# Moving the stationary tiles of the expert stage 64 bytes past a multiple of 512

## The chip, the core and the metric

The kernel runs on one core of one Trainium2 chip. Time is device time in microseconds (us) for one execution of the whole program, and the figure compared is the median of several executions. Times of single instructions are in nanoseconds (ns).

## What is computed

A two-layer encoder on 256 tokens of width 1024, all in float32. Each layer has a mixer with three branches; layer 0 then has a dense feed-forward block and layer 1 a mixture of eight experts. The change touches the expert part alone, so that is what has to be seen:

```python
def swiglu(h, w1, w3, w2):
    return (jax.nn.silu(h @ w1) * (h @ w3)) @ w2

def moe_ffn(h, router, w1, w3, w2):
    logits = (h @ router).astype(jnp.float32)
    top_v, top_i = lax.top_k(logits, TOP_K)
    top_w = jax.nn.softmax(top_v, axis=-1)
    gates = jnp.sum(jax.nn.one_hot(top_i, N_EXPERTS, dtype=jnp.float32) * top_w[..., None], axis=-2)
    y = gates[..., 0:1] * swiglu(h, w1[0], w3[0], w2[0])
    for e in range(1, N_EXPERTS):
        y = y + gates[..., e:e + 1] * swiglu(h, w1[e], w3[e], w2[e])
    return y
```

Every expert has w1 and w3 of 1024 x 3584 and w2 of 3584 x 1024, so the eight together are 336 pieces of 512 x 512 float32 (1 MiB each).

## The kernel before

**Precision.** Float32 products are made of three products of rounded parts. Each operand is split in a high part, rounded to the type fp32r, and a low part, the rest, in the same type. `mm3` (lines 1395 to 1399) multiplies high by high, high by low and low by high into one sum. The first tile argument of `pe.matmul` is the stationary one, which is loaded into the array (128 columns), the second is the moving one, which is streamed (512 columns in the expert stage). Each matmul has its own load of the stationary tile, also where the tile is the same as before.

**Expert stage.** A slot is up to 128 tokens of one expert. Here eight slots run: slot 0 written out, then a loop of seven. The weights of a slot come as 42 units (`UNITS`), each of 512 x 512. SyncE issues one DMA for each into a ring of 14 buffers `eraw` as soon as TensorE has finished the unit 14 before (`eunit_done`). ScalarE copies a unit to its high part `ehi` (line 830, three buffers), VectorE subtracts and writes the low part `elo` over the raw weights (line 1232). TensorE then runs four `mm3` for the unit (line 1736 for w1 and w3, the next branch for w2), 12 matmuls of 512 columns. The moving tiles are always the weights, `ehi` and `elo`. The stationary tiles are the tokens: `hehi` and `helo` (gathered tokens, written by lines 835 and 1277) for w1 and w3, and `eahi` and `ealo` (hidden activations, lines 860 and 1369; `ahi` and `alo` in the code) for w2. Between units TensorE transposes hidden activations (`turn`, line 1442, with the identity matrix held in `tab`), adds the result of the slot before to its tokens (`spread`, line 1711, moving tile `ysb`) and gathers the tokens of the next slot (line 1702, moving tile `Gm`).

**Layer 0 and both mixers.** They use the same `mm3`. In a feature unit (`feature_unit`) the weights are stationary and 256 token columns move; in a token unit (`token_unit`) the tokens `hhi`, `hlo` are stationary and the weights move, 512 or 448 columns of them. The router's product, ahead of the expert stage, has stationary tiles of 8 columns (`rhi`, `rlo`) and 256 moving columns.

**Placement.** All of SBUF that the kernel uses is one arena, whose base is rounded up to a multiple of 512 bytes. `keep` places permanent tiles one after another, each rounded up to 32 bytes; `w` places working tiles at written offsets from `work`, which is rounded up to a multiple of 512. `over_h` is the place of `hhi` (16,384 bytes in), which the expert stage reuses with `hlo` for `hid`, `eahi`, `ealo` and `ysb`. A stationary tile of 128 float32 columns is 512 bytes in each partition, so in the expert stage every tile that a load or a stream reads begins at a multiple of 512. The router's tiles are the exception: `rhi[:, k, :]` begins 32 k bytes past a multiple of 512, `rlo[:, k, :]` 256 bytes further.

Of the kernel before, what the change touches and what calls it, by code (L numbers as in the profile page):

```python
# [19 lines left out]
F32R = mybir.dt.float32r  # L20
# [5 lines left out]
P = 128  # L26
TOKENS, D, DEPTH = 256, 1024, 2
NB = TOKENS // P
KD = D // P
# [16 lines left out]
SLOT = P  # L46
# [97 lines left out]
def encoder(nc, ins, out):  # L144
    ctx = ExitStack()
    with ctx:
# [4 lines left out]
        def at(name, offset, shape, dtype=F32):  # L151
            size = 4
            for n in shape[1:]:
                size *= n
            assert offset + size <= arena_bytes, name
            return nc.alloc_sbuf_tensor_at(name, shape, dtype, offset=base + offset)

        place = [0]

        def keep(name, shape, dtype=F32):  # L160
            size = 4
            for n in shape[1:]:
                size *= n
            t = at(name, place[0], shape, dtype)
            place[0] += -(-size // 32) * 32
            return t
# [4 lines left out]
        over_h = place[0]  # L171
        hhi = keep("hhi", [P, KD, TOKENS], F32R)
        hlo = keep("hlo", [P, KD, TOKENS], F32R)
        tab = keep("tab", [P, T_W])
        bmask = keep("bmask", [P, HEADS, SCORE])
        mmask = keep("mmask", [P, SCORE])
# [17 lines left out]
        def w(name, offset, shape, dtype=F32):  # L194
            return at(name, work + offset, shape, dtype)
# [5 lines left out]
        o = 57344  # L201
# [53 lines left out]
        o = 57344  # L255
# [10 lines left out]
        o = 8192 * (RAW + HI)  # L266
# [3 lines left out]
        eraw = [w(f"eraw{i}", a, [P, 4, 512]) for i, a in enumerate(at_unit)]  # L270
        elo = [w(f"elo{i}", a, [P, 4, 512], F32R) for i, a in enumerate(at_unit)]
        o += 8192 * (E_GATES + E_MERGED)
        hehi = w("hehi", o, [P, KD, SLOT], F32R)
        helo = w("helo", o + 4096, [P, KD, SLOT], F32R)
        Gm = w("Gm", o + 8192, [P, NB, SLOT])
        Gg = w("Gg", o + 9216, [P, NB, SLOT])
        GT = w("GT", o + 10240, [SLOT, NB, P])
        o += 11264

        hid = [at(f"hid{i}", over_h + 2048 * i, [SLOT, FC]) for i in range(2)]  # L280
        ahi = [at(f"eahi{i}", over_h + 4096 + 2048 * i, [P, 4, SLOT], F32R) for i in range(2)]
        alo = [at(f"ealo{i}", over_h + 8192 + 2048 * i, [P, 4, SLOT], F32R) for i in range(2)]
        ysb = at("ysb", over_h + 12288, [SLOT, D])
        place[0] = work + o
        rhi = keep("rhi", [P, KD, NE], F32R)
        rlo = keep("rlo", [P, KD, NE], F32R)
# [1561 lines left out]
```

## Time and profile before

| | |
|---|---|
| median of three runs | 1732.25 us (1731.15 to 1734.08) |
| the profiled execution | 1730.65 us |
| its span, first to last instruction | 1728.8 us |
| TensorE busy (matmuls) | 1677.6 us, 97% |
| VectorE busy | 1270.7 us, 73% |
| ScalarE busy | 1053.4 us, 61% |
| read from HBM | 465.53 MB, 270 GB/s over the span |
| fp32r matmuls in the expert stage | 4032, from 710 to 1716 us |

All rows come from the profiled execution. PE is TensorE's matmuls, PEld its loads of stationary tiles, DVE VectorE, ACT ScalarE, SPq the queue of DMAs that SyncE issues. A matmul's recorded duration holds its way through the array, so consecutive ones overlap; what a matmul costs in a dense row is the distance from its start to the start of the next, called its spacing below. Names are written out<-in; for a matmul the output, then its two inputs, with the moving tile's form behind the array's size.

### The profile page before, as it was taken

To read this page: it belongs to the slowest core of one execution; us is meant where nothing else is said; L and a number is where in the kernel's file an instruction comes from. 1 tells how busy PE (TensorE), PEld (TensorE's weight loads), DVE (VectorE), ACT (ScalarE), POOL (GpSimd) and SP (SyncE) were. 2 spreads that over 40 slices of the span, in tenths; PEclk is the share of its full clock that TensorE was granted. 3 is DMA by queue.
4 is the path that set the end of the run, shared out by engine and by line. 5 is a ranking of instruction groups with operands and counts; after the bars stand their busy time and mean duration, and the time that the engine had idled before them with its cause. 6 is when DMAs were issued, how large, how long until landed. Compare 5 with 4: busy or idle time off the path is not lost.

```text
span 1728.8 us, 23259 instructions
## 1 busy us (share of the span) xinstructions
PE 1677.6 (97%) x9181; PEld 1438.4 (83%) x9181; DVE 1270.7 (73%) x991; ACT 1053.4 (61%) x950; POOL 18.7 (1%) x28
## 2 busy tenths in 40 slices
PE   5999999999899998899999999999999999999997
PEld 4899989999889997678888788788788788788786
DVE  4654565444566466798888888888898898898896
ACT  4364645433536454667667676776676776677675
POOL 1000000000000000000000000000000000000000
PEclk9999999999999999899999999999999999999999
DMA  6643454555654448899999999999999999999980
GB/s 235 208 145 124 147 195 147 183 185 174 209 174 145 137 152 296 313 349 372 323 357 377 316 362 364 323 365 355 327 373 342 337 371 338 344 370 338 346 299 24
DMA packets 234685, 468.52 MB, mean 271 GB/s; under 512 B 7552, under 2 KB 11744, under 8 KB 234624
## 3 DMA queue, kind: packets, MB, share of 16 engines
q1 hardware_dynamic: 232400, 459.17, 76.0%
q0 software_dynamic: 1936, 7.44, 1.2%
q8 instruction: 45, 0.74, 0.2%
q10 hardware_dynamic: 288, 1.05, 0.1%
q14 instruction: 16, 0.13, 0.0%
HBM read 465.53 MB, written 2.10 MB: 270 GB/s over the span
## 4 chain that ended last, share of the span: by engine, by line
PE 92%; DVE 4%; ACT 3%; DMA 1%; issue 1%; SPq 0%; DVEq 0%; ACTq 0%
PE big L1397 21%; PE big L1399 21%; PE big L1398 21%; PE small L1397 7%; PE small L1399 6%; PE small L1398 6%; PE small L1442 2%; DVE elo L1232 2%; PE small L1711 1%; ACT ehi L830 1%; PE small L1702 1%; DMA raw<-w_in 1%; PE small L1591 0%; PE small L1593 0%; PE small L1546 0%
## 5 line engine op out<-in xcount | busy, mean ns | idle before, releaser
L1232 DVE TENSOR_TENSOR elo<-eraw,ehi 128x2048 fp32r<-128x2048 f32 x336 | 769.1, 2295 | 106.5 <-ACT ehi L830 105.2
L830 ACT ACTIVATE ehi<-eraw 128x2048 fp32r<-128x2048 f32 x336 | 643.2, 1918 | 180.8 <-PE big L1399 136.8
L906 DVE TENSOR_TENSOR wlo<-raw,whi 128x2048 fp32r<-128x2048 f32 (+2 forms) x104 | 229.9, 2218 | 206.3 <-ACT whi L628 206.3
L1397 PE MATMUL big<-ehi,hehi 128*128 128x512 f32 x896 | 363.5, 406 | 1.4 <-DVE helo L1277 1.4
L628 ACT ACTIVATE whi<-raw 128x2048 fp32r<-128x2048 f32 (+2 forms) x104 | 192.5, 1858 | 269.8 <-PE big L1399 201.1
L1399 PE MATMUL big<-ehi,helo 128*128 128x512 f32 x896 | 350.0, 391 | 0.0
L1398 PE MATMUL big<-elo,hehi 128*128 128x512 f32 x896 | 349.4, 390 | 0.0
L1397 PE MATMUL big<-hhi,whi 128*128 128x256 f32 x864 | 248.1, 287 | 7.2 <-DVE hlo L926 7.0
L1398 PE MATMUL big<-hlo,whi 128*128 128x256 f32 x864 | 245.7, 284 | 0.0
L1399 PE MATMUL big<-hhi,wlo 128*128 128x256 f32 x864 | 245.7, 284 | 0.0
L1397 PEld LDWEIGHTS big<-ehi,hehi 128*128 128x128 f32 x896 | 168.3, 188 | 40.9 <-issue 5.1
L1398 PEld LDWEIGHTS big<-elo,hehi 128*128 128x128 f32 x896 | 168.5, 188 | 38.0 <-issue 5.0
L1399 PEld LDWEIGHTS big<-ehi,helo 128*128 128x128 f32 x896 | 168.2, 188 | 36.3
L1397 PE MATMUL small<-ehi,eahi 128*128 128x512 f32 x448 | 179.9, 402 | 4.0 <-DVE elo L1232 4.0
L1397 PEld LDWEIGHTS big<-hhi,whi 128*128 128x128 f32 x864 | 167.2, 193 | 10.5 <-DVE hlo L926 8.4
L1399 PE MATMUL small<-ehi,ealo 128*128 128x512 f32 x448 | 174.8, 390 | 0.0
L1398 PE MATMUL small<-elo,eahi 128*128 128x512 f32 x448 | 174.7, 390 | 0.0
L1398 PEld LDWEIGHTS big<-hlo,whi 128*128 128x128 f32 x864 | 167.1, 193 | 0.6 <-issue 0.5
L1399 PEld LDWEIGHTS big<-hhi,wlo 128*128 128x128 f32 x864 | 167.0, 193 | 0.0
L1397 PEld LDWEIGHTS small<-ehi,eahi 128*128 128x128 f32 x448 | 84.2, 188 | 27.1 <-DVE elo L1232 6.4
L1398 PEld LDWEIGHTS small<-elo,eahi 128*128 128x128 f32 x448 | 84.2, 188 | 18.1 <-issue 1.7
L1399 PEld LDWEIGHTS small<-ehi,ealo 128*128 128x128 f32 x448 | 84.1, 188 | 17.8
(292 smaller groups left out, 1698.2 us busy)
## 6 DMA issues: line engine op xcount, KB each, us to landing
eraw<-moe_w SPq DMA_DIRECT2D x336, 1024.0 KB, 5.1
raw<-ffn_w SPq DMA_DIRECT2D x30, 1024.0 KB, 5.0
raw<-w_gate SPq DMA_DIRECT2D x24, 1024.0 KB, 5.0
raw<-w_in SPq DMA_DIRECT2D x20, 1024.0 KB, 5.2
raw<-w_branch SPq DMA_DIRECT2D x12, 1024.0 KB, 4.9
raw<-w_o SPq DMA_DIRECT2D x8, 1024.0 KB, 5.1
raw<-w_in SPq DMA_DIRECT2D x4, 896.0 KB, 5.3
raw<-ffn_w SPq DMA_DIRECT2D x6, 512.0 KB, 3.7
```

The source lines that it names most:

```text
L628: act.activation(whi[u % HI][:, 0:kt, 0:cols], raw[u % RAW][:, 0:kt, 0:cols], ACT.Copy).then_inc(hi_ready, 1)
L830: act.activation(ehi[n % EHI][:, :, :], eraw[n % RING][:, :, :], ACT.Copy).then_inc(ehi_ready, 1)
L906: dve.tensor_tensor(wlo[u % RAW][:, 0:kt, 0:cols], raw[u % RAW][:, 0:kt, 0:cols], whi[u % HI][:, 0:kt, 0:cols].bitcast(F32), ALU.subtract) ...
L1232: dve.tensor_tensor(elo[n % RING][:, :, :], eraw[n % RING][:, :, :], ehi[n % EHI][:, :, :].bitcast(F32), ALU.subtract).then_inc(elo_ready, 1)
L1397: pe.matmul(o, sh, mh, start=start, stop=False, **kw)
L1398: pe.matmul(o, sh, ml, start=False, stop=False, **kw)
L1399: return pe.matmul(o, sl, mh, start=False, stop=stop, **kw)
L1442: return pe.transpose(o, src, ident[0:n, 0:n])
L1702: m = pe.matmul(small[:, gather_bank(s, i), SLOT * k:SLOT * k + SLOT], xn[:, b, (4 * i + k) * P:(4 * i + k + 1) * P], Gm[:, b, :], start=b ...
L1711: pe.matmul(small[:, 3, :], GT[:, i // 2, :], ysb[:, half:half + 512], start=True, stop=True).then_inc(spread_done, 1)
```

## The change

The stationary tiles of the expert stage are placed 64 bytes further: `hehi` and `helo` begin at `o + 64` and `o + 4160`, `eahi` and `ealo` at `over_h + 4160` and `over_h + 8256`, before and after the change each at a distance of 512 or 2048 from one another. `ysb`, the moving tile of `spread`, goes along with them to 64 past a multiple of 512. `Gm`, `Gg`, `GT` and what `keep` places behind them (`rhi` and on) move by a whole 512. To make room behind `ysb`, the permanent tables from `tab` to `rt` move by 64. `ehi`, `elo` and `eraw`, the moving ones, stay at multiples of 512. No instruction, wait, size or order changes.

```diff
@@ -171,6 +171,7 @@
         over_h = place[0]
         hhi = keep("hhi", [P, KD, TOKENS], F32R)
         hlo = keep("hlo", [P, KD, TOKENS], F32R)
+        place[0] += 64
         tab = keep("tab", [P, T_W])
@@ -270,17 +271,18 @@
         o += 8192 * (E_GATES + E_MERGED)
-        hehi = w("hehi", o, [P, KD, SLOT], F32R)
-        helo = w("helo", o + 4096, [P, KD, SLOT], F32R)
+        hehi = w("hehi", o + 64, [P, KD, SLOT], F32R)
+        helo = w("helo", o + 4160, [P, KD, SLOT], F32R)
+        o += 512
         Gm = w("Gm", o + 8192, [P, NB, SLOT])
         Gg = w("Gg", o + 9216, [P, NB, SLOT])
         GT = w("GT", o + 10240, [SLOT, NB, P])
         o += 11264
 
         hid = [at(f"hid{i}", over_h + 2048 * i, [SLOT, FC]) for i in range(2)]
-        ahi = [at(f"eahi{i}", over_h + 4096 + 2048 * i, [P, 4, SLOT], F32R) for i in range(2)]
-        alo = [at(f"ealo{i}", over_h + 8192 + 2048 * i, [P, 4, SLOT], F32R) for i in range(2)]
-        ysb = at("ysb", over_h + 12288, [SLOT, D])
+        ahi = [at(f"eahi{i}", over_h + 4160 + 2048 * i, [P, 4, SLOT], F32R) for i in range(2)]
+        alo = [at(f"ealo{i}", over_h + 8256 + 2048 * i, [P, 4, SLOT], F32R) for i in range(2)]
+        ysb = at("ysb", over_h + 12352, [SLOT, D])
         place[0] = work + o
```

## Rows read from the trace of the kernel before

**Rows 1.** The page's second part: 40 slices of the span, busy tenths of each.

```profile
PE   5999999999899998899999999999999999999997
PEclk9999999999999999899999999999999999999999
DMA  6643454555654448899999999999999999999980
```

**Rows 2.** Busy time by stretch (us, then busy us of each engine, clock, DMA).

```profile
740.00:1690.00 950.00, 946.41 (x4324) 772.53 (x4323) 823.49 (x530) 672.92 (x446) 0.00 (x0) 1.00 0.97 346
```

**Rows 3.** The same view, the busiest five us of DMA, where the ring is filled.

```profile
700.00:705.00 5.00, 3.81 (x17) 3.75 (x18) 2.62 (x8) 0.49 (x2) 0.00 (x0) 0.51 1.05 409
```

**Rows 4.** Waits, 740 to 1690 us: engine, line <- releaser: total us, times, longest.

```profile
ACT ehi L830 <- PE big L1399: 128.1, 198, 1.7
DVE elo L1232 <- ACT ehi L830: 97.2, 166, 1.1
...
PE small L1397 <- DVE elo L1232: 3.6, 10, 0.9
...
SPq L543 <- PE big L1399: 490.1, 208, 3.1
```

**Rows 5.** Timeline of PE in the expert stage (start us, us): 25 starts, first and last.

```profile
937.12 0.39 PE L1397 MATMUL big<-ehi,hehi 128*128 128x512 f32 x1
...
942.57 0.39 PE L1397 MATMUL big<-ehi,hehi 128*128 128x512 f32 x1
```

**Rows 6.** Timeline of PEld in the same stretch: the loads beside the matmuls.

```profile
937.81 0.19 PEld L1398 LDWEIGHTS big<-elo,hehi 128*128 128x128 f32 x1
938.04 0.19 PEld L1399 LDWEIGHTS big<-ehi,helo 128*128 128x128 f32 x1
```

**Rows 7.** Timeline of PE, a feature unit of 256 moving columns: 22 starts.

```profile
399.98 0.28 PE L1397 MATMUL big<-hhi,whi 128*128 128x256 f32 x1
...
402.50 0.28 PE L1397 MATMUL big<-hhi,whi 128*128 128x256 f32 x1
```

**Rows 8.** Timeline of PE, a token unit of 448 moving columns: nine starts.

```profile
59.83 0.36 PE L1397 MATMUL big<-whi,hhi 128*128 128x448 f32 x1
...
61.45 0.36 PE L1399 MATMUL big<-whi,hlo 128*128 128x448 f32 x1
```

**Rows 9.** Timeline of PE, the router's product: stationary tiles of eight columns.

```profile
692.66 0.28 PE L1397 MATMUL small<-hhi,rhi 128*8 128x256 f32 x1 [2.21 <-issue]
692.78 0.28 PE L1398 MATMUL small<-hlo,rhi 128*8 128x256 f32 x1
692.89 0.28 PE L1399 MATMUL small<-hhi,rlo 128*8 128x256 f32 x1
693.01 0.28 PE L1397 MATMUL small<-hhi,rhi 128*8 128x256 f32 x1
693.13 0.28 PE L1398 MATMUL small<-hlo,rhi 128*8 128x256 f32 x1
693.25 0.34 PE L1399 MATMUL small<-hhi,rlo 128*8 128x256 f32 x1
```

**Rows 10.** Timeline of PE, plain float32 matmuls in a row (xcount, merged).

```profile
98.95 3.40 PE L1546 MATMUL small<-cqnT,wuq 128*128 128x256 f32 x15
849.39 1.02 PE L1711 MATMUL small<-ysb,GT 128*128 128x512 f32 x2
87.15 0.82 PE L1442 MATMUL small<-tab,csb 128*128 128x128 f32 x6
1074.45 1.95 PE L1702 MATMUL small<-Gm,xn 128*128 128x128 f32 x16
```

**Rows 11.** Groups of instructions, 740 to 1690 us: writers of weights and stationary tiles.

```profile
L830 ACT ACTIVATE ehi<-eraw 128x2048 fp32r<-128x2048 f32 x318 | 609.1, 1918 | 170.8 <-PE big L1399 128.1 <-PE small L1399 42.8
L1232 DVE TENSOR_TENSOR elo<-eraw,ehi 128x2048 fp32r<-128x2048 f32 x319 | 728.6, 2290 | 98.4 <-ACT ehi L830 97.2
L1369 DVE TENSOR_TENSOR ealo<-small,eahi 128x512 fp32r<-128x512 f32 x53 | 36.4, 687 | 22.0 <-ACT eahi L860 22.0
L1277 DVE TENSOR_TENSOR helo<-small,hehi 128x512 fp32r<-128x512 f32 x14 | 9.6, 687 | 5.6 <-ACT hehi L835 5.6
```

## Prediction

> **What bounds the kernel now.** I read first the 40 slices of the page, then the busy time by stretch, then the waits, and last the timeline of TensorE alone, because the change alters nothing but addresses and only the timeline shows what one access costs. The slices say that TensorE is at nine tenths nearly everywhere and its clock at full speed, 2.4 GHz [rows 1]. In the heart of the expert stage it is busy for 946.4 of 950 us at a granted clock of 1.00, beside DMA at 0.97 of its time and 346 GB/s [rows 2]. Two engines look full there, so the waits decide. Each DMA issue waits for TensorE to finish a unit (490 us in the larger of two groups), ScalarE waits for TensorE to free a buffer of the high part (128 us), VectorE waits for ScalarE (97 us), and TensorE waits for VectorE for a few us in all [rows 4]. DMA is therefore paced by TensorE; it has been seen at 409 GB/s while the ring was filled [rows 3]. TensorE is the bound, and the expert stage is 4032 matmuls of fp32r, 12 for each of 336 units. Whatever a placement does to one of them is multiplied by 4032.
>
> **What one of them costs.** From the start at 937.12 to the one 24 later at 942.57 lie 5.45 us, a spacing of 227.1 ns [rows 5]. At 2.4 GHz 512 columns take 213.3 ns, so 13.8 ns are on top. The load of the next stationary tile begins within 0.01 us of a matmul and lies wholly under it (0.19 us recorded) [rows 5, 6], so its reading and the streaming run side by side. The same sum elsewhere, all with loads of 128 columns and at the same residue modulo 512: 256 moving columns come every 2.52 / 21 = 120.0 ns, 13.3 above their 106.7 [rows 7], and 448 every 1.62 / 8 = 202.5 ns, 15.8 above their 186.7 [rows 8]. Plain float32 matmuls are streamed at half the rate. Their 15 with 256 columns are (3.40 - 0.38) / 14 = 215.7 ns apart, where 213.3 would be the bare stream (0.38 is the recorded duration of one) [rows 10]. So a stream of fp32r pays some 11 ns per matmul that a float32 one with an equal load does not. This is what the change can reach, if reading both tiles from the same place modulo 512 is its cause.
>
> **Is it the cause?** The trace has one test of it. The router's product loads 8 columns and not 128, and its tiles begin at 0, 256, 32 and 288 bytes past a multiple of 512 in turn, with the moving tile at 0. Its starts at full clock, 692.66 to 693.25, give 0.59 / 5 = 118 ns, every single one 110 to 120 as far as two decimals tell [rows 9]. That is 11.3 ns above the stream of 106.7. A load with a sixteenth of the reads keeps 11.3 of the 13.3 ns, and four different residues give the same. A collision of the two reads should have shrunk with the load, or changed with the residue. What goes with the load's length is 13.3 - 11.3 = 2 ns. Against this weighs that 64 is not among the four residues, that all four might fall on the same banks, and that 8 columns are a short load. The row nearest to the disputed thing speaks for a fixed cost of changing the stationary tile under a fast stream, so I take nothing.
>
> **The change part by part.** Removed and added instructions: none; DMAs and waits: none; queue orders: the same.
> The stationary tiles at residue 64, 4032 matmuls: taken as 0. Lower bound: all that fp32r pays above float32, 227.1 - 215.7 = 11.4 ns each [rows 5, 10], 4032 x 11.4 = 46 us. Upper bound: the worst addition seen for any fp32r stream, 15.8 - 13.3 = 2.5 ns [rows 7, 8], 4032 x 2.5 = 10 us.
> The identity in `tab`, now at 64, moving tile of each transpose: they are (0.82 - 0.27) / 5 = 110 ns apart, where a gather of the same size without transposing takes (1.95 - 0.27) / 15 = 112 [rows 10]. The bare stream is 106.7, so with the 224 of the hidden activations and some 200 others between -1.4 and +0.8 us; I take 0.
> `ysb` at 64, moving tile of 56 matmul records in the loop, of which two take 1.02 us, their starts 0.43 apart [rows 10]. The bare stream is 427 ns, so nothing can be gained; an fp32r-like charge of 11 ns would be 0.6 us. I take 0.
> Writes of the moved tiles: the low part of activations and that of the gathered tokens take 687 ns each, though they lie in two different regions [rows 11]. Copies of 512 columns do not feel where they land, and DMA touches none of the moved tiles but small tables once. Tables from `tab` to `rt` already begin at assorted multiples of 32 (the three behind `tab` at 96 past a multiple of 512, by their sizes), so ScalarE and VectorE read such addresses now. 0.
> The sum is 1730.65 + 0 = 1730.65 us for the profiled execution, with its small terms -1.4 to +1.4. The median of the runs is 1.6 us above that execution, so the forecast is 1732 us.
>
> **A rule weighed.** The rows show 227.1 ns for a spacing with a load wholly beside it [rows 5, 6]. The Trainium skill, page TensorE: Matmul & The Clock Gate, section on what each phase of a matmul is for, says that TensorE has two independent read ports and that "Loading the next tile's weights doesn't steal SBUF read bandwidth from the running matmul." By that rule the placement does nothing and the sum stays 1732. The same page, section Wait — 56ns, not 53.3ns?, puts the fixed cost of a warm matmul at 2.5 ns, an estimate of 215.8 ns for 512 columns; the float32 row agrees, the fp32r rows do not, by 11 ns. If those 11 ns were a theft the first rule denies, the sum would be the faster rival's.
>
> **Rival 1, faster: the reads do collide.** Load and stream begin together at the same residue in every one of the 4032, and the fp32r stream reads twice as many bytes in a microsecond as the float32 one, which pays next to nothing. If a shift of 64 bytes keeps the two on different banks, up to 11.4 ns go. For it: the gap between fp32r and float32, and that no residue of 64 has been timed. Against it: the 8-column row. What is late next: a buffer freed by TensorE takes 1.92 + 2.29 = 4.21 us through ScalarE and VectorE [rows 11], and TensorE meanwhile has two units of 12 x 227.1 ns = 2.73 us, 5.45 us; at 215.7 ns it would have 5.18, still 0.97 to spare. VectorE needs 2.29 us and its smaller work out of the 3.0 us that a unit now takes on average (950 / 318), and 2.9 would do. DMA would have to give 346 x 3.0 / 2.86 = 363 GB/s, against the 409 seen. So nearly all of it arrives; I take off 2 us for the few places where TensorE already waits for VectorE [rows 4] and have 46 - 2 = 44 us: 1688 us. A partial gain, the 2 ns that do go with the load's length, would be 8 us: 1724 us.
>
> **Rival 2, slower: the load now crosses a boundary.** A stationary tile of 512 bytes at a multiple of 512 lies in one block of that size; 64 bytes on it reaches into two, on all 4032 loads. If fetching a second block costs as the odd length of 448 columns seems to cost the stream, 2.5 ns come on top, 10 us in all: 1742 us. It decides from 0.9 ns a matmul on (3.5 us). For it: lengths that are no multiple of 256 columns do pay [rows 8]. Against it: the load is hidden for all but the start of the next matmul, and the router's loads at 32 and 288 are no slower.
>
> **Rival 3: the change does not do what it says.** The base is rounded to 512 and the working tiles' offset stays at 45,056 by the sizes, so the residues are as written. Were the placement undone, the time would be 1732 too; I count it with no change.
>
> **How the numbers follow.** No change, 0.42, with its own range 1730 to 1735. Faster, 0.38: two thirds of it near the full 1688, the rest between it and 1728. Slower, 0.20: three quarters at 1736 to 1746 around 1742, the rest beyond, since a collision that equal residues happen to avoid has no row that bounds it. About 0.2%, 3.5 us, is what a measurement of this kernel can tell from no change. The range 1686 to 1746 holds the three cases but for that last piece and the deepest gains.
>
> **What would show it.** In the expert stage the spacing between consecutive starts is the whole test: 227 ns for no change, 216 for the full collision, about 225 for the part, 229.6 for the crossing. The layers before must be the same to within a us: their spacing 227, 120 and 202.5. The transposes at 110 and the spread at 0.43 us show whether `tab` and `ysb` matter. If the spacing falls and the time does not, TensorE's waits for `elo`, or issues of SPq that no longer wait for TensorE, say which of the two took its place. The prediction is wrong at its root if the spacing moves by more than a ns.

## The result and the profile after

The changed kernel takes 1751.08 us (median, 1749.98 to 1752.79) against 1731.70 us for the kernel before. The ratio is 1.0111, 95% interval 1.0094 to 1.0129: slower by 1.1%, some 19 us, outside the range given. Its profiled execution has a span of 1750.1 us, 21.3 more than before.

The page's first two rows of slices and the busy time by stretch (us, then busy us and count of each engine, clock, DMA share, GB/s) of the changed kernel:

```profile
PE   5999999999999997999999999999999999999997
PEclk8999999999999999999999999999999999999999
...
740.00:1690.00 950.00, 947.29 (x4239) 756.59 (x4238) 808.11 (x521) 659.12 (x436) 0.00 (x0) 1.00 0.98 343
```

TensorE is as busy as before and its clock as full, but in the 950 us of the expert stage it ran 4239 matmul records and not 4324 [rows 2]. Nothing new waits. Of the waits of the same stretch (engine, line <- releaser: total us, times, longest) those for TensorE grow, and behind them that of VectorE for ScalarE (108.2 for 97.2 us), while TensorE waits for VectorE for less than before (2.7 for 3.6 us, [rows 4]):

```profile
ACT ehi L832 <- PE big L1401: 137.9, 194, 1.7
DVE elo L1234 <- ACT ehi L832: 108.2, 168, 1.1
...
PE small L1399 <- DVE elo L1234: 2.7, 10, 0.7
```

The cause stands in the timeline of TensorE, 25 starts of the changed kernel (first and last), which answer to [rows 5]:

```profile
911.23 0.39 PE L1399 MATMUL big<-ehi,hehi 128*128 128x512 f32 x1
...
916.83 0.39 PE L1399 MATMUL small<-ehi,eahi 128*128 128x512 f32 x1
```

That is 5.60 / 24 = 233.3 ns where it was 227.1. The writers of the moved tiles did not change (687 and 688 ns for the low parts, [rows 11]). Where the whole time went is seen from the first and the last matmul of the low weights (duration ns min/median/max, first and last start us), the first two rows before, the last two after:

```profile
L1398 PE MATMUL big<-elo,hehi x896: 387/389/398, 710.7 to 1700.0; 128*128 128x512 f32 x180
L1398 PE MATMUL small<-elo,eahi x448: 387/389/398, 733.6 to 1715.6; 128*128 128x512 f32 x150
```

```profile
L1400 PE MATMUL big<-elo,hehi x896: 388/394/398, 711.8 to 1721.1; 128*128 128x512 f32 x180
L1400 PE MATMUL small<-elo,eahi x448: 392/394/398, 734.9 to 1736.8; 128*128 128x512 f32 x150
```

The stage was 1715.6 - 710.7 = 1004.9 us and is 1736.8 - 711.8 = 1025.0, so 20.1 of the 21.3 us lie in it, 5.0 ns for each of 4032 matmuls; the other 1.1 us lie ahead of it. It is 5.0 and not 6.2 for two reasons. The 25 starts read before were among the quickest: over the whole stage, taking from the starts every spacing below 240 ns, the mean was 227.8 and is 233.3 ns, 5.5 more. And the spacings from 240 ns on, where TensorE pauses or does other work between units, shrank a little, from 57.7 us in all (135 of them) to 54.1 (126). The median recorded duration rose with the spacing, from 389 to 394 ns. A grouped row can show that, but it marks a spacing of 233 ns alone: a kernel further below has 229.2 ns at a median of 388.

### The profile page after: what moved, and what is told of

Its sections match the earlier page's. It is cut to its first block, busy times and chain, and to the rows that moved or that the text cites. A ratio compares the mean times of both kernels' runs of the same rounds, so it can differ in the third digit from the quotient of the medians.

```text
span 1750.1 us, 23259 instructions
## 1 busy us (share of the span) xinstructions
PE 1699.0 (97%) x9181; PEld 1439.4 (82%) x9181; DVE 1272.0 (73%) x991; ACT 1053.9 (60%) x950; POOL 18.7 (1%) x28
## 4 chain that ended last, share of the span: by engine, by line
PE 92%; DVE 3%; ACT 2%; DMA 1%; issue 0%; SPq 0%; DVEq 0%; ACTq 0%
PE big L1399 21%; PE big L1400 21%; PE big L1401 21%; PE small L1399 7%; PE small L1400 7%; PE small L1401 7%; PE small L1444 2%; DVE elo L1234 2%; PE small L1713 1%; ACT ehi L832 1%; PE small L1704 1%; DMA raw<-w_in 1%; PE small L1593 0%; PE small L1595 0%; PE small L1548 0%
## 5 line engine op out<-in xcount | busy, mean ns | idle before, releaser
L1399 PE MATMUL big<-ehi,hehi 128*128 128x512 f32 x896 | 367.2, 410 | 1.4 <-DVE helo L1279 1.4
L1401 PE MATMUL big<-ehi,helo 128*128 128x512 f32 x896 | 353.8, 395 | 0.0
L1400 PE MATMUL big<-elo,hehi 128*128 128x512 f32 x896 | 353.7, 395 | 0.0
```

Of the source, the lines that this page charges most:

```text
L1399: pe.matmul(o, sh, mh, start=start, stop=False, **kw)
L1400: pe.matmul(o, sh, ml, start=False, stop=False, **kw)
L1401: return pe.matmul(o, sl, mh, start=False, stop=stop, **kw)
```

## Experiments

Two theories stood first. R: what counts is how the residue of the stationary tile stands to that of the moving one. B: the stationary tile reaches over a boundary of 512 bytes and its load costs more, as the slower rival had it. s and m below are the bytes by which the stationary and the moving tile lie past a multiple of 512.

### A bench of residues

Not the encoder. Its engine program runs rows of 40 matmuls of fp32r, in the order high, high, low of the stationary tile and high, low, high of the moving one, each with its own load. While the rows run no other engine works and the DMA share is 0.00. It ran once.

```python
for i in range(ROUNDS):
    k = i // 3
    lo = (0, 0, 1)[i % 3]
    ml = (0, 1, 0)[i % 3]
    a = P * (k % 2 + 2 * lo) + s % 32 // 4
    b = 512 * (k % 2 + 2 * ml) + m % 32 // 4
    q = pe.matmul(ps[c % 2][0:ld, 0:cols], st[:, a:a + ld], mv[:, b:b + cols], ...)
```

> Not the encoder: a bench that only runs rows of 40 fp32r matmuls with their loads, one row for each pair of residues modulo 512 of stationary tile (s) and moving tile (m); its output is not the reference's. Theory R (what counts is the difference of the two residues): s=0 m=0 gives a spacing of 227 ns for 512 columns, s=64 m=0 gives 233, s=64 m=64 and s=256 m=256 give 227 again, and s=0 m=64 differs from 227 too. Theory B (a stationary tile that reaches over a boundary of 512 costs more, whatever moves): every s other than 0 gives 233, s=64 m=64 too, and every m with s=0 gives 227. With loads of 8 columns both expect s=0 and s=64 within 1 ns of each other if the cost goes with the load's length; if the cost is paid at the start of the two reads, 8 columns show it in full.

The timeline of its TensorE; a row is (start us, time of all, moving and stationary tile named by their residue, stationary columns, moving columns, count). A spacing is (time of all - 0.39) / 39, 0.39 being the recorded duration of one.

```profile
33.27 9.23 PE L88 MATMUL ps<-m0x,s0x 128*128 128x512 f32 x40
42.34 9.24 PE L88 MATMUL ps<-m0x,s16x 128*128 128x512 f32 x40
51.41 9.49 PE L88 MATMUL ps<-m0x,s32x 128*128 128x512 f32 x40
60.74 9.50 PE L88 MATMUL ps<-m0x,s64x 128*128 128x512 f32 x40
...
79.43 9.44 PE L88 MATMUL ps<-m0x,s128x 128*128 128x512 f32 x40
88.71 9.32 PE L88 MATMUL ps<-m0x,s192x 128*128 128x512 f32 x40
97.87 9.24 PE L88 MATMUL ps<-m0x,s256x 128*128 128x512 f32 x40
106.95 9.49 PE L88 MATMUL ps<-m0x,s320x 128*128 128x512 f32 x40
...
144.06 9.31 PE L88 MATMUL ps<-m64x,s0x 128*128 128x512 f32 x40
...
180.94 9.48 PE L88 MATMUL ps<-m448x,s0x 128*128 128x512 f32 x40
190.26 9.25 PE L88 MATMUL ps<-m64x,s64x 128*128 128x512 f32 x40
...
255.97 9.40 PE L88 MATMUL ps<-m0x,s0x 128*8 128x512 f32 x40
265.21 9.43 PE L88 MATMUL ps<-m0x,s64x 128*8 128x512 f32 x40
274.48 9.36 PE L88 MATMUL ps<-m0x,s0x 128*64 128x512 f32 x40
283.68 9.47 PE L88 MATMUL ps<-m0x,s64x 128*64 128x512 f32 x40
```

At m=0 the stationary residues 0, 16 and 256 give 226.7 to 226.9 ns, 32, 64 and 320 give 233.3 to 233.6, 128 gives 232.1 and 192 gives 229.0. With s=0, a moving residue of 64 gives 228.7, as s=192 does, and 448 gives 233.1, as s=64 does. Equal residues of 64 give 227.2. Rows of the same s - m modulo 256 agree within 1.5 ns throughout, and s=0 and s=64 run again at the end give 227.2 and 233.3. So the spacing goes by s - m, and it repeats every 256 bytes: theory R. B falls, since equal residues of 64 reach over the boundary and cost nothing. The bench has the encoder's 227 and 233 with no DMA and no other engine at work, so those have no part in it. The last four rows concern the test on which the prediction rested. With loads of 8 columns the spacing is 231.0 at s=0 and 231.8 at s=64: it hardly feels the residue, and it is higher than the 226.7 of a full load. With 64 columns it is 230.0 and 232.8. So what the residue of 64 costs does grow with the load, 0.8, 2.8 and 6.9 ns for 8, 64 and 128 columns, while the spacing at equal residues falls.

### Both kinds of tile at 64

```diff
-        ehi = [w(f"ehi{i}", 8192 * i, [P, 4, 512], F32R) for i in range(EHI)]
+        ehi = [w(f"ehi{i}", 64 + 8192 * i, [P, 4, 512], F32R) for i in range(EHI)]
...
-        at_unit = [o + 8192 * i for i in range(E_GATES + E_MERGED)]
-        at_unit += [8192 * (EHI + i) for i in range(RING - E_GATES - E_MERGED)]
+        at_unit = [64 + o + 8192 * i for i in range(E_GATES + E_MERGED)]
+        at_unit += [64 + 8192 * (EHI + i) for i in range(RING - E_GATES - E_MERGED)]
...
```

> The changed kernel with ehi, elo and eraw at 64 past a multiple of 512 too, so that stationary and moving tiles have the same residue again and each stationary tile still reaches over a boundary of 512. Theory R (difference of residues): spacing back at 227 ns, 1732 us. Theory B (boundary of the stationary tile): spacing stays at 233 ns, 1751 us.

1731.91 us against 1731.00, ratio 1.0003 (0.9994 to 1.0013). The whole loss is gone while every stationary tile still lies at 64. The median recorded duration is back at 389 ns, and the spacings below 240 ns average 228.1. In the encoder too it is the relation of the two.

### The stationary tiles back, the rest left moved

`hehi`, `helo`, `eahi`, `ealo` at multiples of 512; `tab` and what follows it, and `ysb`, stay at 64. Against the changed kernel:

```diff
-        hehi = w("hehi", o + 64, [P, KD, SLOT], F32R)
-        helo = w("helo", o + 4160, [P, KD, SLOT], F32R)
+        hehi = w("hehi", o, [P, KD, SLOT], F32R)
+        helo = w("helo", o + 4096, [P, KD, SLOT], F32R)
...
-        ahi = [at(f"eahi{i}", over_h + 4160 + 2048 * i, [P, 4, SLOT], F32R) for i in range(2)]
-        alo = [at(f"ealo{i}", over_h + 8256 + 2048 * i, [P, 4, SLOT], F32R) for i in range(2)]
+        ahi = [at(f"eahi{i}", over_h + 4096 + 2048 * i, [P, 4, SLOT], F32R) for i in range(2)]
+        alo = [at(f"ealo{i}", over_h + 8192 + 2048 * i, [P, 4, SLOT], F32R) for i in range(2)]
```

> The changed kernel with hehi, helo, eahi and ealo back at multiples of 512; the tables from tab on and ysb stay at 64 past one. Theories R and B both: spacing 227 ns, 1732 us. Theory T (the moved tables or the spread's moving tile are to blame): 1745 us or more with a spacing near 227 in the dense rows.

1731.21 us, ratio 1.0000 (0.9990 to 1.0009). Tables, identity and `ysb` cost nothing that can be measured, as the prediction's small terms had it.

### Only the gathered tokens moved

The lower half of that edit alone: `eahi` and `ealo` back at multiples of 512, `hehi` and `helo` at 64.

```diff
-        ahi = [at(f"eahi{i}", over_h + 4160 + 2048 * i, [P, 4, SLOT], F32R) for i in range(2)]
+        ahi = [at(f"eahi{i}", over_h + 4096 + 2048 * i, [P, 4, SLOT], F32R) for i in range(2)]
...
```

> The changed kernel with eahi and ealo back at multiples of 512, hehi and helo at 64 past one: two thirds of the 4032 matmuls keep the moved stationary tile. Both R and B: 6 ns on 2688 of them, 16 us less what waits hide, so 1745 us; the matmuls into small (w2) at 227 ns, those into big at 233.

1746.01 us, ratio 1.0085 (1.0068 to 1.0101): 15.0 us for two thirds of the matmuls, where 16 less what waits hide were expected. The rows of this kernel show the two kinds side by side, w1 and w3 with the longer duration, w2 with the old one (their spacings below 240 ns average 233.3 and 228.5):

```profile
L1400 PE MATMUL big<-elo,hehi x896: 391/394/398, 712.0 to 1715.5; 128*128 128x512 f32 x180
L1400 PE MATMUL small<-elo,eahi x448: 387/389/402, 735.0 to 1731.1; 128*128 128x512 f32 x150
```

### The roles swapped

The moving tiles at 64 as in the kernel with both kinds at 64, the stationary ones at multiples of 512:

```diff
-        hehi = w("hehi", o + 64, [P, KD, SLOT], F32R)
-        helo = w("helo", o + 4160, [P, KD, SLOT], F32R)
-        o += 512
+        hehi = w("hehi", o + 512, [P, KD, SLOT], F32R)
+        helo = w("helo", o + 4608, [P, KD, SLOT], F32R)
+        o += 1024
...
```

> The changed kernel with the roles swapped: ehi, elo and eraw at 64 past a multiple of 512, hehi, helo, eahi and ealo at multiples of 512. If any unequal residues cost the same: 233 ns, 1751 us. If the signed difference s - m modulo 256 counts, as the first bench has it (192: 228.9 ns against 227.2 at 0): 4032 times 1.7 ns, 7 us on 1731, so 1738 us.

1735.89 us against 1731.65, ratio 1.0027 (1.0017 to 1.0036). The loss is 4 us and not 19: the sign of the difference counts. The stage shows it too:

```profile
L1400 PE MATMUL big<-elo,hehi x896: 387/388/398, 710.8 to 1705.1; 128*128 128x512 f32 x180
L1400 PE MATMUL small<-elo,eahi x448: 387/388/398, 733.8 to 1720.7; 128*128 128x512 f32 x150
```

It lasts 1720.7 - 710.8 = 1009.9 us, 5.0 more than before, and its spacings below 240 ns average 229.2 ns, as the bench's rows at 192 do, against 227.8 before. That is 1.4 ns, 5.6 us on 4032 matmuls; the 7 us expected took 1.7 ns from the bench, whose own 226.7 to 227.2 at equal residues the encoder does not quite reach.

### 256 in place of 64

Tables, stationary tiles and `ysb` at 256 past a multiple of 512:

```diff
-        place[0] += 64
+        place[0] += 256
-        hehi = w("hehi", o + 64, [P, KD, SLOT], F32R)
+        hehi = w("hehi", o + 256, [P, KD, SLOT], F32R)
...
```

> The changed kernel with 256 in place of 64: stationary tiles, ysb and tables 256 past a multiple of 512. Difference modulo 256: 0, spacing 227, 1732 us. A rule modulo 512, or a boundary of 512 that is crossed: 233 ns, 1751 us.

1730.81 us against 1731.51, ratio 0.9996 (0.9986 to 1.0006). The encoder repeats every 256 bytes as the bench does.

### A bench of lengths, and tiles that alternate

The same bench with other residues and numbers of columns, and two rows in which the residues alternate from one matmul to the next:

```diff
-                st, mv = views["s", s], views["m", m]
                 for i in range(ROUNDS):
+                    s, m = both(ss)[i % 2], both(ms)[i % 2]
+                    st, mv = views["s", s], views["m", m]
```

> A second bench, no encoder, its output is not the reference's: rows of 40 fp32r matmuls, stationary residues in steps of 16 bytes at m=0 for 256 and 512 moving columns, some other lengths, and two rows that alternate. If the spacing depends on the difference s - m modulo 256, s=0 m=64 at 256 columns equals s=192 m=0. Alternating tiles tell which pair counts. Row (s0 with m0, s64 with m64): 227 ns if a matmul's own two tiles count, and about 231 (the mean of 233.4 and 228.9) if what counts is the load that runs beside a stream, which is the load of the next matmul. Row (s64 with m0, s0 with m64): about 231 if the own pair counts, 227 if the load beside the stream counts. For 256 columns the first bench gave 113.7 at s=64 and 120 at 0 and 256; a theory that every unequal residue costs expects no value below 120 elsewhere.

At 512 columns the finer steps show a shelf and not a slope: 0 and 16 at 226.9, everything from 32 to 160 between 232.1 and 234.4, 192 at 229.2, 224 at 233.3. The rows of 256 columns, for which 0.28 us is the duration of one:

```profile
24.29 4.95 PE L94 MATMUL ps<-m0x,s0x 128*128 128x256 f32 x40
...
33.81 4.89 PE L94 MATMUL ps<-m0x,s32x 128*128 128x256 f32 x40
...
43.26 4.70 PE L94 MATMUL ps<-m0x,s64x 128*128 128x256 f32 x40
...
62.09 4.96 PE L94 MATMUL ps<-m0x,s128x 128*128 128x256 f32 x40
...
71.69 4.87 PE L94 MATMUL ps<-m0x,s192x 128*128 128x256 f32 x40
```

Here equal residues are among the worst, (4.95 - 0.28) / 39 = 119.7 ns, and s=64 the best, 113.3; 192 gives 117.7. With 192, 320 and 384 columns all four residues tried lie within 3.5 ns of one another, and equal ones cost no more than 0.7 ns over the best. At 448 columns 192 is the best, 200 ns against 203 at equal residues, and at 480 it is 64, 216 against 217. The two alternating rows begin at 326.72 and 335.98 and the next row at 345.31:

```profile
326.72 0.40 PE L94 MATMUL ps<-m0x,s0x 128*128 128x512 f32 x1
...
335.98 0.39 PE L94 MATMUL ps<-m0x,s64x 128*128 128x512 f32 x1
...
345.31 0.40 PE L94 MATMUL ps<-m0x,s0x 128*128 128x512 f32 x1
```

The row whose own pairs are equal takes 9.26 / 40 = 231.5 ns, as it should if what counts is the load that runs beside a stream, which is that of the next matmul. Its two kinds of start differ as that reading wants, 233.5 ns on average from a stream at 0 and 229.5 from one at 64. The opposite row should then have 227 and takes 9.33 / 40 = 233.3, which neither reading gives. For tiles that alternate the rule is open; the difference is a rule for rows of constant residues. So that load and stream get in each other's way is the likely reason for it, but no run shows it.

### The gain of 256 columns, in the mixer

The kernel before, with one line more; `work` stays at a multiple of 512, so the expert stage keeps equal residues. Feature units then have s - m = 64 modulo 256, token units 192.

```diff
         over_h = place[0]
+        place[0] += 192
         hhi = keep("hhi", [P, KD, TOKENS], F32R)
```

> The kernel before with hhi and hlo at 192 past a multiple of 512 and the expert stage as before. In feature units s - m is then 64 modulo 256, for 2592 matmuls of 256 columns; in token units it is 192 for 576 of 448 or 512. Theory of the difference, with the bench's figures: 2592 times 6.2 ns gained, 576 times 1.7 lost, so 15 us faster, 1716 us, spacing 113.7 in feature units. Rival, that any departure from equal residues costs in a real kernel: 1732 or more. Rival, that the weights' path bounds these units: spacing 113.7 within a unit and the time unchanged.

1722.12 us against 1731.65, ratio 0.9940 (0.9926 to 0.9953): faster by 9.5 us where 15 were expected. The timeline says why. These are 22 starts each of feature units with the same tiles at the same residues, in the mixer of layer 0 and in its dense block:

```profile
29.96 0.28 PE L1398 MATMUL big<-hhi,whi 128*128 128x256 f32 x1
...
32.34 0.28 PE L1398 MATMUL big<-hhi,whi 128*128 128x256 f32 x1
```

```profile
270.18 0.28 PE L1398 MATMUL big<-hhi,whi 128*128 128x256 f32 x1
...
272.65 0.28 PE L1398 MATMUL big<-hhi,whi 128*128 128x256 f32 x1
```

2.38 / 21 = 113.3 ns in the first, 2.47 / 21 = 117.6 in the second, against 120.0 before [rows 7]. Most units of the mixer of layer 0 have the first value and some the second; in the dense block all have the second. Over all feature units on `hhi` and `hlo` the spacings below 140 ns average 116.0 ns for 119.9 before, so 3.9 ns on 2592 matmuls, 10 us, and the token units take back some 0.6 of it.

### The branch products too

`ahi`, `alo`, `bhi`, `blo`, `chi` and `clo`, moving tiles of 576 more matmuls, at 192 as well (with 256 bytes of room behind the first four):

```diff
-        bhi[0], blo[0] = w("ahi", o, [P, 4, TOKENS], F32R), w("alo", o + 4096, [P, 4, TOKENS], F32R)
+        bhi[0], blo[0] = w("ahi", o + 192, [P, 4, TOKENS], F32R), w("alo", o + 4288, [P, 4, TOKENS], F32R)
...
-        o += 16384
+        o += 16640
```

> As mixer_moving_192 and the moving tiles of the branch products (ahi, alo, bhi, blo, chi, clo) at 192 too, 576 more matmuls of 256 columns: 3.5 us on top, 1713 us.

1716.79 us against 1731.65, ratio 0.9912 (0.9897 to 0.9927), where 1713 were expected: the step before had already fallen short by 6 us. This step gave 5.3 us and not 3.5. The spacings of the 576 matmuls fell from 120 to 113.4 ns, which is 3.8 us; what the other 1.5 are, no run shows. It is the fastest of all the kernels run, 15 us under the kernel before and 34 under the changed one. The expert stage has kept its length (first and last start of the low weights' matmuls, 696.8 and 1701.3: 1004.5 us) and begins 13.9 us earlier:

```profile
L1399 PE MATMUL big<-elo,hehi x896: 387/389/398, 696.8 to 1685.7; 128*128 128x512 f32 x180
L1399 PE MATMUL small<-elo,eahi x448: 387/389/402, 719.7 to 1701.3; 128*128 128x512 f32 x150
```

### The opposite sign in the mixer

`hhi` and `hlo` at 64, against the kernel before:

```diff
         over_h = place[0]
+        place[0] += 64
```

> The kernel before with hhi and hlo at 64 and not at 192: in feature units s - m is 192 modulo 256, in token units 64. By the benches: 2592 matmuls of 256 columns at 117.8 for 120.0 ns, 5.7 us gained, 480 of 512 columns at 233.3 for 227.1, 3 us lost, so 1729 us. If only the size of the difference counted and not its sign, as much as mixer_moving_192 gave: 1722.

1728.61 us against 1731.51, ratio 0.9981 (0.9971 to 0.9990), as the bench's figures gave it. The sign counts here as well.

### Does the spacing remember?

The third bench repeats rows of 30 with one thing or another between them:

```python
for s, m, cols in BASES:
    made.append((s, m, cols, 128, 30))
    for kind in ("448", "64", "load8", "idle", "plain", "twelve"):
        made.append(kind)
        made.append((s, m, cols, 128, 30))
```

> A third bench, no encoder, its output is not the reference's: six pairs of residues, each as seven rows of 30 fp32r matmuls, with something else between the rows (one matmul of 448 columns, one of 64, one with a load of 8, an idle time until ScalarE has copied, one plain float32 matmul, twelve of 480 columns). Theory H (the spacing has a memory: the phase of loads against streams, set by what went before, persists): rows of the same pair differ after different breaks, s=0 m=192 at 256 columns between 113.4 and 117.8 ns, as in the feature units of the mixer kernels. Theory C (conditions in the encoder, its DMA and the other engines' traffic, make the two values): all rows of a pair agree within 0.5 ns, none of that traffic being there.

The first seven rows are all s=0, m=192, 256 columns; what stands between them is the break:

```profile
19.36 3.70 PE L87 MATMUL ps<-m192x,s0x 128*128 128x256 f32 x30
22.90 0.36 PE L87 MATMUL ps<-m0x,s0x 128*128 128x448 f32 x1
23.09 3.59 PE L87 MATMUL ps<-m192x,s0x 128*128 128x256 f32 x30
...
30.04 0.39 PE L87 MATMUL ps<-m0x,s0x 128*8 128x512 f32 x1
30.27 3.57 PE L87 MATMUL ps<-m192x,s0x 128*128 128x256 f32 x30
...
34.95 3.69 PE L87 MATMUL ps<-m192x,s0x 128*128 128x256 f32 x30
```

(3.70 - 0.28) / 29 = 117.9, then 114.1, then 113.4, then 117.6 ns: the same tiles, the same program for 30 matmuls, and two values, by what went before. s=64, m=0 has the same two in its own seven rows. After at most five starts a row has its value, and it keeps it to its end. The break alone does not decide: after the idle time s=0, m=192 has the upper value and s=64, m=0 the lower one. At 512 columns there is nothing of the kind: 233.0 to 233.5 ns for s=64, 226.7 to 227.6 for equal residues and 228.8 to 229.2 for s=192, in the rows whose first spacing is not a long one of some 310 ns. Theory C, which would have made traffic of the encoder the cause, falls: there is none here. Of theory H, what is shown for 256 columns is that the value depends on what went before; that it is a phase of loads against streams is not shown. It agrees with why the mixer gained 9.5 us and not 15: its units fall into either value and keep it to their end. What sets the value was not found.

## Why the prediction was wrong

**What bounds the kernel.** Right. TensorE paced the expert stage, and a placement was multiplied by 4032. Of 5.5 ns each, 22 us, 20 arrived; the longer spacings between units gave back the rest.

**What one matmul costs.** Right in its numbers, wrong in its use. The spacing of 227 ns was read well, but float32 rows were taken to show what is free of the effect. No residue tried at 512 columns came below 226.7 ns, so the 11 ns above float32 are not what a placement can reach; at 256 columns, 6.4 of the 13.3 above the bare stream are.

**"Is it the cause?"** This is the step that failed. It argued from loads of 8 columns, at residues 0, 256, 32 and 288, that a collision "should have shrunk with the load, or changed with the residue". The first two benches ran that case at residue 64: loads of 8 columns stay within 0.8 ns between s=0 and s=64 at 512 moving columns, where full loads go from 226.7 to 233.6, and at 256 they have 116.7 at both, where full loads go from 119.7 to 113.3. The effect of the residue does shrink with the load, as the text supposed, but then a load of 8 columns shows next to nothing of it and says nothing about a long one. What remained at 8 columns was no fixed cost that a full load pays as well: at 512 columns 8 loaded columns are slower (231.0) than 128 (226.7), at 256 they are quicker (116.7 against 119.7). So the subtraction 13.3 - 11.3 = 2 ns did not give what goes with the load's length. The text did name the two gaps, that 64 was untimed and 8 columns short, and then gave them too little weight.

**The change part by part.** The upper bound was mis-sized: 2.5 ns, from the odd length of 448 columns, for what measured 6.2 between the 25 starts before and after and 5.0 over the stage, so 20 us and not 10. The row was of another length at equal residues; it bounded nothing about unequal ones. All the other parts at 0 were right, as the kernel with the stationary tiles back shows.

**The rule weighed.** By the Trainium skill, page TensorE: Matmul & The Clock Gate, section on what each phase is for, the load takes no read bandwidth from the running matmul, and the prediction concluded from it that the placement does nothing. That conclusion fails: the residue of the loaded tile alone, everything else unchanged, moves the spacing by some 7 ns, in a bench where nothing else runs. The measurement decides. By the Trainium skill, page SBUF — State Buffer, section Specifications (TRN2), SBUF has lines of 16 bytes and each crossing to a new one costs something. Neither what the bench shows, that 16 bytes are free and 32 are not, nor the period of 256 bytes comes out of that, and no run here shows such lines.

**The rivals.** The slower one had the sign and, at 1742, half the size, by a wrong mechanism: no boundary is involved. The faster one looked in the right place, at how load and stream lie to each other, with the wrong sign: equal residues at 512 columns are the best case and not the worst. At 256 columns, where 64 bytes gave 113.3 or 117.7 for 119.7, the sign would have been right.

**The range.** It ended at 1746 with a note that a collision which equal residues avoid had no row to bound it. That was the case that came, with a chance of 0.05. No row of the kernel before bounds what unequal residues cost, so the bound of 10 us was not one, and a range that ends at it claimed more than the rows gave.

## What to carry to other kernels

For fp32r matmuls of 512 columns place stationary and moving tiles at equal residues modulo 256 bytes; for 256 columns let the stationary tile lie 64 bytes past the moving one. Both hold for rows in which all tiles of a kind have one residue. Measure it for your own lengths in a bench of a few rows, since the best residue differs by length and the spread is 3% at 512 columns and nearly 6% at 256. Do not infer the cost of a full load from a row with a short one: subtract only rows that differ in the one thing that is asked.

## What was not expected of the hardware

The spacing of fp32r matmuls depends on s - m modulo 256, with its sign: 226.7 ns at 0, 233.6 at 64, 229.0 at 192 for 512 columns. At 256 columns the order turns round: 119.7 at 0, 113.3 or 117.9 at 64. Those last two are both held by the same row of instructions until it ends, and which of them comes depends on what ran before. What the residue costs grows with the load's length: 0.8 ns with 8 loaded columns, 2.8 with 64, 6.9 with 128, at 512 moving ones. The time that a shorter load gives back can be negative: 231.0 ns with 8 loaded columns against 226.7 with 128.
